# Causal masks of an attention moved from VectorE's reduction into a bf16 matmul, and 32-row value matmuls for the compressed branch

## The reference

```
proj = rmsnorm(x) @ w_in            # queries, 6 K/V streams, gates, u, v, 2 merge gates of 2048
kc, vc = compress_blocks(...)       # 31 compressed tokens for each of 4 groups
# 16 heads in 4 groups, head width 64, query blocks of 128
s_c = q @ kc.T;  p_c = masked_softmax(s_c, cmp_end <= t)
s_s = q @ k_sel.T; p_s = masked_softmax(s_s, pos <= t)      # top 16 blocks of 64: here all of them
s_w = q @ k_w.T;   p_w = masked_softmax(s_w, kpos <= t, window 512)
A = g0 * p_c @ vc + g1 * p_s @ v_sel + g2 * p_w @ v_w
```

## Time and profile before

| | |
|---|---|
| median of 3 runs (lowest to highest) | 3020.6 us (3016.07 to 3021.23) |
| profiled execution, time | 3020.6 us |
| profiled execution, span | 3018.9 us |
| TensorE matmul, busy share of the span | 97% |
| VectorE, ScalarE, GpSimd, busy share | 52%, 21%, 27% |
| mean granted TensorE clock | 0.993 of full speed |
| TensorE's share of the chain that ended last | 88% |

### The profile page before, as it was taken

The page is one execution under the profiler, slowest core; times in us unless marked ns, Lnnn a source line. Parts: engine busy times, 40 slices in busy tenths (PEclk is TensorE's granted clock), DMA queues, the critical chain, the costliest instruction groups (busy, mean ns, idle before and its releaser), DMA issues.

```text
span 3018.9 us, 39451 instructions
## 1 busy us (share of the span) xinstructions
PE 2935.1 (97%) x13845; PEld 2433.6 (81%) x13845; DVE 1579.2 (52%) x2833; ACT 628.8 (21%) x1394; POOL 800.0 (27%) x638
## 2 busy tenths in 40 slices
PE   6999999999999999998989999999999999999997
PEld 5887888888888788887768888888888888888886
DVE  4434666666555575448584444444444444444454
ACT  3011444444212332112231111000111100011111
POOL 0100333333105553113162222111222211122232
PEclk9999999999999999999999999999999999999999
DMA  6323322223334545334123333333333333333332
GB/s 194 94 77 75 88 76 82 83 79 84 105 99 104 160 133 139 107 101 126 56 84 97 97 94 94 94 95 96 97 97 97 97 98 97 97 97 97 89 105 99
DMA packets 543164, 300.56 MB, mean 100 GB/s; under 512 B 9076, under 2 KB 533480, under 8 KB 541672
## 3 DMA queue, kind: packets, MB, share of 16 engines
q1 hardware_dynamic: 532768, 285.63, 34.3%
q10 hardware_dynamic: 10312, 13.83, 1.4%
HBM read 286.84 MB, written 12.58 MB: 99 GB/s over the span
## 4 chain that ended last, share of the span: by engine, by line
PE 88%; DVE 5%; DMA 2%; POOL 2%; issue 1%; ACT 1%; ACTq 0%; SPq 0%; DVEq 0%; POOLq 0%
PE bank L549 28%; PE bank L551 27%; PE bank L550 27%; DVE w_lo L929 1%; PE bank L715 1%; DVE w_hi L927 1%; PE bank L685 1%; DMA rows_bc<-in_sgu_b_dram 1%; PE bank L700 1%; DVE act_lo L1164 1%; DVE bank L1028 1%; PE bank L613 0%; PE bank L795 0%; DVE prob_t L1047 0%; PE bank L680 0%
## 5 line engine op out<-in xcount | busy, mean ns | idle before, releaser
L549 PE MATMUL bank<-act_hi,w_hi 128*128 128x512 f32 x2832 | 1123.1, 397 | 7.2 <-DVE act_lo L1164 4.0
L551 PE MATMUL bank<-act_hi,w_lo 128*128 128x512 f32 x2832 | 1105.8, 390 | 0.0
L550 PE MATMUL bank<-act_lo,w_hi 128*128 128x512 f32 x2832 | 1105.5, 390 | 0.0
L927 DVE CAST w_hi<-raw 128x512 fp32r<-128x512 f32 (+1 forms) x996 | 493.7, 496 | 1161.1 <-PE bank L551 1135.0
L929 DVE TENSOR_TENSOR w_lo<-raw,w_hi 128x512 fp32r<-128x512 f32 (+1 forms) x996 | 788.3, 791 | 34.3
L551 PEld LDWEIGHTS bank<-act_hi,w_lo 128*128 128x128 f32 x2832 | 531.4, 188 | 114.5
L549 PEld LDWEIGHTS bank<-act_hi,w_hi 128*128 128x128 f32 x2832 | 532.0, 188 | 109.0 <-DVE act_lo L1164 5.1
L550 PEld LDWEIGHTS bank<-act_lo,w_hi 128*128 128x128 f32 x2832 | 532.5, 188 | 98.1 <-issue 0.2
L549 PE MATMUL bank<-ff_hi,w_hi 128*128 128x512 f32 x704 | 275.3, 391 | 0.0
L551 PE MATMUL bank<-ff_hi,w_lo 128*128 128x512 f32 x704 | 274.1, 389 | 0.0
L550 PE MATMUL bank<-ff_lo,w_hi 128*128 128x512 f32 x704 | 274.0, 389 | 0.0
(11 more groups left out here) (231 smaller groups left out, 2693.1 us busy)
## 6 DMA issues: line engine op xcount, KB each, us to landing
raw<-in_w_ffn_in_dram SPq DMA_DIRECT2D x88, 1024.0 KB, 5.6
raw<-in_w_in_dram SPq DMA_DIRECT2D x68, 1024.0 KB, 5.7
raw<-in_w_ffn_out_dram SPq DMA_DIRECT2D x32, 1024.0 KB, 5.8
raw<-in_w_mix_out_dram SPq DMA_DIRECT2D x16, 1024.0 KB, 6.1
raw<-in_w_ffn_out_dram SPq DMA_DIRECT2D x16, 768.0 KB, 5.0
merge_gates<-gate_out ACTq DMA_DIRECT2D x32, 256.0 KB, 2.0
raw<-in_w_proj_a_dram SPq DMA_DIRECT2D x16, 512.0 KB, 4.3
raw<-in_w_proj_b_dram SPq DMA_DIRECT2D x16, 512.0 KB, 5.5
```

What stands on the lines that cost most here:

```text
L549: pe.matmul(dst, w_hi[:, q, j, 0:m], hi, start=first, stop=False)
L550: pe.matmul(dst, w_hi[:, q, j, 0:m], lo, start=False, stop=False)
L551: return pe.matmul(dst, w_lo[:, q, j, 0:m], hi, start=False, stop=last)
L927: dve.tensor_copy(w_hi[:, q, :, 0:width], src).then_inc(hi_done, 1)
```

## The change

The causal mask of items 1 to 4 moves to TensorE: a bf16 tile `causal_b` (128 by 128, 0 and -1e30) is put into the diagonal block of the bank by one more matmul with `ident_b`, ahead of the two score matmuls, which now add to it. VectorE's instruction becomes a plain maximum that only reads the bank. The signs turn: queries are scaled by plus 1/8, the reductions are negated maxima, the exponential has scale 1. The cost of these steps in `step_cost` grows by 64 (times 4). The buffer `pc_t` goes: the compressed probabilities use 32 rows of `prob_t`, and `vc_hl` has 32 rows, so that the two value matmuls of the compressed branch contract over 32 rows. The waits for `pc_t`'s clearing and for the masks go with them.

```diff
-        cost += 5 * 64 if step % PARTS == 0 else 2 * max(64, 64 * (qi + 1) + 8)
+        cost += 5 * 64 if step % PARTS == 0 else 64 + 2 * max(64, 64 * (qi + 1) + 8)
...
-        vc_hl = at("vc_hl", [P, GROUPS, P], F32R, C + 38 * KIB)
-        pc_t = at("pc_t", [P, 2, 2 * P], F32R, C + 32 * KIB)
+        vc_hl = at("vc_hl", [NCP, GROUPS, P], F32R, C + 38 * KIB)
...
+        causal_b = const("causal_b", [P, P], BF16)
...
-        causal = at("causal", [P, T], F32, spot[0] - T * 4)
...
+                    pe.matmul(s[:, qi * P:n], ident_b[:], causal_b[:], start=True, stop=False, skip_group_check=True)
                     for w in range(2):
-                        mm = pe.matmul(s[:, 0:n], q_hl[:, hu % 2, e, w], k_hl[:, b, j, 0:n], start=w == 0, stop=w == 1)
+                        mm = pe.matmul(s[:, 0:n], q_hl[:, hu % 2, e, w], k_hl[:, b, j, 0:n], start=False, stop=w == 1, skip_group_check=True)
...
-                        mm = pe.matmul(o, vc_hl[:, j], pc_t[:, w], start=w == 0, stop=False)
+                        mm = pe.matmul(o, vc_hl[:, j], prob_t[0:NCP, n % 2, w, 0:2 * P], start=w == 0, stop=False)
...
-            dve.wait_ge(masks_made, 3)
...
-                        dve.tensor_reduce(attn_max[:, hu % 2, 0:2], s[:, 0:2 * NCP].rearrange("p (e n) -> p e n", e=2), AX.X, ALU.min).then_inc(max_done, 1)
+                        dve.tensor_reduce(attn_max[:, hu % 2, 0:2], s[:, 0:2 * NCP].rearrange("p (e n) -> p e n", e=2), AX.X, ALU.max, negate=True).then_inc(max_done, 1)
                     else:
-                        n = (qi + 1) * P
-                        dve.tensor_tensor_reduce(out=s[:, 0:n], in0=s[:, 0:n], in1=causal[:, T - n:T], scale=1.0, scalar=-MASKED,
-                                                 op0=ALU.add, op1=ALU.min, accum_out=attn_max[:, hu % 2, part + 1:part + 2]).then_inc(max_done, 1)
+                        dve.tensor_reduce(attn_max[:, hu % 2, part + 1:part + 2], s[:, 0:(qi + 1) * P], AX.X, ALU.max, negate=True).then_inc(max_done, 1)
...
-                    if k == 0:
-                        dve.tensor_tensor(pc_t[0:NCP, 1], bank[4 + n % 2][0:NCP, 0:2 * P], pc_t[0:NCP, 0].bitcast(F32), ALU.subtract).then_inc(p_lo, 1)
-                    else:
-                        dve.tensor_tensor(prob_t[:, n % 2, 1, 0:cols_n], bank[4 + n % 2][:, 0:cols_n],
-                                          prob_t[:, n % 2, 0, 0:cols_n].bitcast(F32), ALU.subtract).then_inc(p_lo, 1)
+                    dve.tensor_tensor(prob_t[0:rows, n % 2, 1, 0:cols_n], bank[4 + n % 2][0:rows, 0:cols_n],
+                                      prob_t[0:rows, n % 2, 0, 0:cols_n].bitcast(F32), ALU.subtract).then_inc(p_lo, 1)
...
-                    act.activation(q_t[:, ds(i * 2 + u, 1), :], result(ph, i, u)[:], ACT.Copy, scale=-HD ** -0.5).then_inc(banks_read, 1)
+                    act.activation(q_t[:, ds(i * 2 + u, 1), :], result(ph, i, u)[:], ACT.Copy, scale=HD ** -0.5).then_inc(banks_read, 1)
...
-            act.wait_ge(pads_zero, 3)
...
-            pool.wait_ge(cmp_out, 2)
-            pool.memset(pc_t[:].bitcast(F32), 0.0).then_inc(pads_zero, 1)
```

More of the change, by code:

```diff
@@ L1041, in _ @@
                     n = TURN_BASE[own] + k
-                    cols_n = 2 * P * len(turns(HALVES[own][2])[k])
+                    rows, cols_n = (NCP, 2 * P) if k == 0 else (P, 2 * P * len(turns(HALVES[own][2])[k]))
                     dve.wait_ge(p_hi, n + 1)
-                    if k == 0:
-                        dve.tensor_tensor(pc_t[0:NCP, 1], bank[4 + n % 2][0:NCP, 0:2 * P], pc_t[0:NCP, 0].bitcast(F32), ALU.subtract).then_inc(p_lo, 1)
-                    else:
-                        dve.tensor_tensor(prob_t[:, n % 2, 1, 0:cols_n], bank[4 + n % 2][:, 0:cols_n],
-                                          prob_t[:, n % 2, 0, 0:cols_n].bitcast(F32), ALU.subtract).then_inc(p_lo, 1)
+                    dve.tensor_tensor(prob_t[0:rows, n % 2, 1, 0:cols_n], bank[4 + n % 2][0:rows, 0:cols_n],
+                                      prob_t[0:rows, n % 2, 0, 0:cols_n].bitcast(F32), ALU.subtract).then_inc(p_lo, 1)
                 if step - 1 in CLOSE_AT:
@@ L1313, in _ @@
                             a = act.activation(prob_c[:, hu % 2, e * NCP:(e + 1) * NCP], s[:, e * NCP:(e + 1) * NCP], ACT.Exp,
-                                               bias=attn_max[:, hu % 2, e:e + 1], scale=-1.0, accum_out=den[:, hu % 2, 3 * e:3 * e + 1])
+                                               bias=attn_max[:, hu % 2, e:e + 1], accum_out=den[:, hu % 2, 3 * e:3 * e + 1])
                     else:
@@ L1317, in _ @@
                         n = (qi + 1) * P
-                        a = act.activation(prob[:, hu % 2, part - 1, 0:n], s[:, 0:n], ACT.Exp, bias=attn_max[:, hu % 2, part + 1:part + 2], scale=-1.0,
+                        a = act.activation(prob[:, hu % 2, part - 1, 0:n], s[:, 0:n], ACT.Exp, bias=attn_max[:, hu % 2, part + 1:part + 2],
                                            accum_out=den[:, hu % 2, 3 * e + b:3 * e + b + 1])
@@ L1323, in _ @@
                     n = TURN_BASE[own] + k
-                    cols_n = 2 * P * len(turns(HALVES[own][2])[k])
+                    rows, cols_n = (NCP, 2 * P) if k == 0 else (P, 2 * P * len(turns(HALVES[own][2])[k]))
                     act.wait_ge(p_turned, n + 1)
                     wait(act, pv_step, n - 1)
[L1327 to L1330, removed]
+                    act.activation(prob_t[0:rows, n % 2, 0, 0:cols_n], bank[4 + n % 2][0:rows, 0:cols_n], ACT.Copy).then_inc(p_hi, 1)
                 if part == 1 and hu + 1 < len(HALVES):
@@ L1579, in _ @@
                                    pattern=[[-1, P]], channel_multiplier=1).then_inc(ident_made, 1)
-            pool.memset(causal[:], 0.0).then_inc(masks_zero, 1)
+            pool.memset(causal_b[:], 0.0).then_inc(masks_zero, 1)
             pool.memset(cmp_mask_b[:], 0.0).then_inc(masks_zero, 1)
@@ L1585, in _ @@
             pool.wait_ge(masks_zero, 3)
-            diagonal = causal[:, T - P:T]
-            pool.affine_select(out=diagonal, in_=diagonal, compare_op=ALU.is_ge, fill=-MASKED, base=0,
+            pool.affine_select(out=causal_b[:], in_=causal_b[:], compare_op=ALU.is_ge, fill=MASKED, base=0,
                                pattern=[[-1, P]], channel_multiplier=1).then_inc(masks_made, 1)
-            pool.affine_select(out=cmp_mask_b[:], in_=cmp_mask_b[:], compare_op=ALU.is_ge, fill=-MASKED, base=1 - CMP_LEN,
+            pool.affine_select(out=cmp_mask_b[:], in_=cmp_mask_b[:], compare_op=ALU.is_ge, fill=MASKED, base=1 - CMP_LEN,
                                pattern=[[P, TC], [0, 2], [-CMP_STEP, NCP]], channel_multiplier=1).then_inc(masks_made, 1)
```

## The result

The changed kernel takes 3045.1 us (median of 4 runs, 3041.9 to 3046.2) against 3020.5 before, a ratio of 1.0083 with a 95% interval of 1.0065 to 1.0100: slower by 24.6 us. The forecast was slower by 11.1 (3031.7), in a range up to 3044. The sign was right, the size was not, and the time lies just outside the range.

The account below looks back on a forecast made before the run. TensorE was taken to bound the kernel, busy 97% of the span. Masks +16.6 us less 5.5 given back by late places made +11.1 on 3020.6, so 3031.7 us, range 3021 to 3044.

Parts of the forecast that it names:

- TensorE bounds the stretch, a matmul added there costs its slot: Attention interleaved with merge-gate tiles: TensorE busy 475.8 of 480.1 us, so an added instruction costs its full slot.
- The mask matmuls, +16.6 us: Window and selected scores: 128 added bf16 mask matmuls on TensorE at 0.13 us each, 16.6 us.
- unlike widths: Transposes at 0.11 us and 128-column scores at 0.115 each, read as weight loads setting the pace of small matmuls.
- Rival C: Mask and first score loads pulled ahead, each mask costing only its 0.0575 us stream; not slower, 3021.7 us; chance 0.13.
- VectorE's reduction: Window and selected maxima: plain reduction about 0.69 us at 512 columns, as long as the masked; accumulator reads go, 17.9 us.
- Its relief gives back 5.5 of 6.3 us: VectorE earlier by 0.7 us a half and TensorE later by 0.5 close most late places, -5.5 us.
- late places: Ten value matmuls near the ends of the query chunk 3 halves, starting late behind VectorE's low halves; 6.3 us in sum.
- The compressed branch's values, taken at no change in slot: Compressed-branch value matmuls, 64 in all, contracting over 32 rows instead of 128, taken to cost nothing more.
- B: Switching to 32-row value pairs and back drains the array 32 times, +10.2 us, 3041.9 us in all; chance 0.22.
- D: The 32-row value pairs overlap with their neighbours, -7.4 us on top, 3024.3 us with the mask forecast; chance 0.04.
- The half-clock entry stays as it is: Attention entry: the 6.2 us half-clock stretch stays, its cause, waits before the first scores, being untouched.
- The rest at nothing: Clearing of `pc_t`, waits on it and on the mask, and moved gate tiles were taken to cost nothing.

Follow-up runs that it names:

- m128_nomask: m128 without its 128 mask matmuls, so window and selected scores are not masked at all and output differs; 3016.6 us, 0.9985 of the kernel before.
- addmask: The kernel before plus one bf16 matmul of zeros ahead of each of 128 score pairs, VectorE's masked reduction kept; 3034.7 us.
- m128: The changed kernel with the compressed-branch value pair contracted over all 128 rows again, masks still on TensorE; 3034.5 us, 1.0046 of the kernel before.

## Why the prediction came out as it did

*TensorE bounds the stretch, a matmul added there costs its slot.* Right: TensorE was busy 494.65 of 495.10 us afterwards, and the masks cost what their slots do.

*The mask matmuls, +16.6 us.* Right: 0.12 to 0.14 us each, 16.3 in all. The price came from a row of another shape and held. Parts of its working did not. The "unlike widths" from which it read that the load sets the pace are both 128 columns; the trace bears the reading out all the same, with 0.236 us for a pair of 256-column scores. And the bf16 load that isn't pulled ahead is not what costs: with a float32r mask it is pulled ahead, and 0.01 us is all that this saves. Rival C is refuted by the same rows: no mask cost its stream of 0.0575 us alone.

*VectorE's reduction.* Right in the duration (684 ns for 690), wrong in what leaves VectorE: the records of the reads add up to 17.9 us, but they lie under their neighbours, and busy time fell by 3.1 us (6.6 in m128_nomask). There are also four reads in a half, not five. *Its relief gives back 5.5 of 6.3 us.* This step failed. It took VectorE to be behind through its own work, so that reads gone would make it 0.7 us earlier; the late places are the end of a chain through ScalarE in which VectorE idles 1.33 us, and the reads were hidden. With the relief and the moved tiles 0.6 us came back (m128_nomask, 6.3 to 5.7). This is near the prediction's own sign of failure, late places that stay open "because ScalarE, not VectorE, sets them". What closes late places is TensorE coming later: masks with VectorE as before give 2.9 (addmask), masks with VectorE relieved and the tiles moved give the same 2.9 (m128). In the forecast the two were added, 0.7 and 0.5 us a half, and nearly all of the 6.3 was to vanish. In the changed kernel 5.2 us did, so that the 5.5 looks right, but this is luck: the height switches added delay of their own. As a credit it is 3.4 us for the masks without them.

*The compressed branch's values, taken at no change in slot.* This is the step that failed and that put the time outside the range. It was read as "columns and stationary width stay", and a row of 128-row matmuls stood for one of 32 rows. Four runs show 0.39 us for each switch in and out, at 32 and at 64 rows, for one matmul or two between the switches: 12.5 us. The bound for B, 10.2 us from the modelled tail of a matmul (0.32 us a pair for 0.39), was near. B was the right case and had a chance of 0.22; its sum of 3041.9 lacks 2.3 us on the switches. D, an overlap, is refuted, as both ways in and out got longer. The Trainium skill, "TensorEngine Tiling (Array Packing)", Key Properties, says that a change of tiling mode drains the engine. The traces agree in that each change of height costs, 0.39 us for the way there and back; that the array drains is not to be seen in them. That page of the Trainium skill lists modes by the width of the stationary tile too. Here a change of width passes at no extra cost.

*The half-clock entry stays as it is.* It did not in the profiled execution, which is why the spans differ by 21.1 us. What the prediction calls its cause, the waits before the first scores (1.54 and 0.42 us), stands unchanged ahead of a full-clock entry. The medians differ by 24.6, and the profiled execution lies near the lower end of the changed kernel's runs; that gap of 3.5 us is within the spread between executions of one kernel (3041.9 to 3046.2).

*The rest at nothing.* Nothing in the trace speaks against it: the stretch behind the attention took 2225.5 and 2224.9 us.

With the switches at 12.5 and a credit of 5.2, the same sum gives 3020.6 + 16.3 + 12.5 - 5.2 = 3044.2 us.

## What to carry to other kernels

Where TensorE is the bound, look at the height of every small matmul: cutting the contraction to the rows that carry data saved no TensorE time here and cost 0.39 us at each place between full-height neighbours, at 32 rows as at 64; zero rows and full height are cheaper. Moving a mask from a VectorE at 67% to a TensorE at 99% pays about 0.13 us a mask for something that had been hidden. And stalls in which the bound engine waits for another are not given back one for one when that other gets faster: test relief and cover apart before counting both. Before crediting an engine with a shorter instruction, see whether it idles just ahead of the late result, and whether the instruction's record lies under its neighbour's: 17.9 us of recorded reads were worth 3 to 7 us of busy time here.

## What was not expected of the hardware

A height of 64 rows costs as much as 32 (0.635 us a pair both, 0.245 at 128), and the cost is not borne at the entry alone: 0.09 us on the way in, 0.19 on the pair's end, 0.11 on the product behind. A matmul with a bf16 stationary operand had its load start with it, not under the one before (31.9 us of idle loader before 119 of 128), while the float32r one was loaded ahead; yet the two differ by 0.01 us a matmul. VectorE's accumulator read has a record of 140 ns, but the next instruction starts at the same time as the read, so that it takes about 0.01 us of the queue. After the same idle stretch ahead of the attention, some profiled executions spend about 6 us at or near 1.2 GHz (granted 0.50 to 0.61 over 6.2 us) and others none, worth 2.3 to 2.8 us.
